# Compression and index scores in one stage, and row maxima taken from masked products

## The reference

```
def compress(k_raw, pe, w1, b1, w2):                   # 31 blocks of 32 tokens, stride 16
    flat = (k_raw[:, idx] + pe).reshape(B, n_cmp, G, 32 * 64)
    return silu(flat @ w1 + b1) @ w2                   # w1: 2048 x 256, w2: 256 x 64

o_cmp: softmax over the 31 compressed keys; o_sel, o_win: softmax over tokens up to t
# index scores of the second kind, 4 heads of 64
logits = einsum('bthd,bsd->bths', qi, ki) / 8
score = einsum('bths,bth->bts', relu(logits), wi / 2)  # masked where s > t
_, idx = top_k(score, 128)                             # the keys that a token attends to
o_dsa = softmax(q @ k[idx] / 8) @ v[idx]
```

## Time and profile before

| | |
|---|---|
| median of 3 runs | 3341.09 us (3338.08 to 3343.44) |
| the profiled execution | 3344.92 us |
| its span, first to last instruction | 3343.1 us |
| mean granted TensorE clock | 0.961 |
| TensorE busy | 3132.5 us (94%) |
| VectorE, ScalarE, GpSimd busy | 1796.5, 857.9, 123.3 us |

### The profile page before, as it was taken

The page is one execution under the profiler, slowest core; times in us unless marked ns, Lnnn a source line. Parts: engine busy times, 40 slices in busy tenths (PEclk is TensorE's granted clock), DMA queues, the critical chain, the costliest instruction groups (busy, mean ns, idle before and its releaser), DMA issues. The chain is left out here.

```text
span 3343.1 us, 42238 instructions
## 1 busy us (share of the span) xinstructions
PE 3132.5 (94%) x17720; PEld 2650.7 (79%) x17720; DVE 1796.5 (54%) x2690; ACT 857.9 (26%) x1051; POOL 123.3 (4%) x96
## 2 busy tenths in 40 slices
PE   7856878999999998999999999999999999899998
PEld 6745436888888886778888888888888886698997
DVE  4647663664655656546545433764645555553434
ACT  3322434421211122314212111421212223132222
POOL 2320221000000000000000000000000000000000
PEclk9975878999999999999999999999999999999999
DMA  4343002343434312113333221342433220232331
GB/s 132 93 121 117 1 0 76 101 126 101 126 113 120 107 45 69 42 51 89 94 94 94 95 60 54 114 145 82 125 101 97 85 68 2 92 89 88 90 96 54
DMA packets 340318, 288.30 MB, mean 86 GB/s; under 512 B 12896, under 2 KB 315488, under 8 KB 339168
## 3 DMA queue, kind: packets, MB, share of 16 engines
q1 hardware_dynamic: 340192, 286.58, 28.8%
HBM read 279.72 MB, written 2.10 MB: 84 GB/s over the span
## 5 line engine op out<-in xcount | busy, mean ns | idle before, releaser
L2117 PE MATMUL PS<-x_hi_f,w_lo 128*128 128x258 f32 (+2 forms) x2560 | 622.3, 324 | 0.0
L2117 PE MATMUL PS<-x_lo_f,w_hi 128*128 128x258 f32 (+2 forms) x2560 | 622.0, 324 | 0.0
L2117 PE MATMUL PS<-x_hi_f,w_hi 128*128 128x258 f32 (+2 forms) x2560 | 620.8, 323 | 0.8 <-DVE w_lo L2165 0.8
L2117 PEld LDWEIGHTS PS<-x_hi_f,w_hi 128*128 128x128 f32 x2560 | 395.4, 189 | 43.9 <-issue 1.5
L2117 PEld LDWEIGHTS PS<-x_hi_f,w_lo 128*128 128x128 f32 x2560 | 395.3, 189 | 42.0
L2117 PEld LDWEIGHTS PS<-x_lo_f,w_hi 128*128 128x128 f32 x2560 | 393.2, 189 | 40.5
L2132 ACT ACTIVATE w_hi<-w_raw 128x2048 fp32r<-128x2048 f32 x131 | 250.0, 1908 | 498.3 <-PE PS L2117 488.8
L2117 PE MATMUL PS<-hid_hi_f,w_hi 128*128 128x512 f32 x1232 | 341.4, 347 | 0.9 <-DVE hid_lo_f L2185 0.9
L2117 PE MATMUL PS<-hid_hi_f,w_lo 128*128 128x512 f32 x1232 | 341.5, 347 | 0.0
L2117 PE MATMUL PS<-hid_lo_f,w_hi 128*128 128x512 f32 x1232 | 339.0, 345 | 0.0
L2143 ACT ACTIVATE silu_a_f<-silu_a_f,shift_out_f 128x512 f32<-128x512 f32 (+1 forms) x154 | 90.2, 626 | 928.7 <-DVE silu_a_f L2176 928.7
(11 more groups left out here) (336 smaller groups left out, 4335.4 us busy)
## 6 DMA issues: line engine op xcount, KB each, us to landing
w_raw<-in_w_ffn_dram SPq DMA_DIRECT2D x240, 512.0 KB, 5.0
sq_f<-in_w_ada_dram SPq DMA_DIRECT2D x128, 512.0 KB, 3.5
w_raw<-in_w_in_dram SPq DMA_DIRECT2D x46, 512.0 KB, 5.0
w_raw<-in_w_out_dram SPq DMA_DIRECT2D x24, 512.0 KB, 5.5
w_raw<-in_w_ffn_dram SPq DMA_DIRECT2D x32, 384.0 KB, 3.9
ada_room<-in_w_ada_dram SPq DMA_DIRECT2D x16, 512.0 KB, 3.4
ada_s<-in_conditions_dram SPq DMA_DIRECT2D x4, 1024.0 KB, 5.0
hT<-hT SPq DMA_DIRECT2D x56, 64.0 KB, 2.0
```

Source lines behind the costliest of these rows:

```text
L2117: last = nc.tensor.matmul(c.PS[:, 4 * q + 2 * w + m, 0:e - a], wt, xt[:, a:e], start=first, stop=end)
```

## The change

- The weights of the key compression are loaded into the ring's two slots at the end of `project_first`. The other tables are loaded at the start of the compression, small ones first; both tables of `attend_first` too.
- `compress` and `index_scores` become one block. The shifted copies are made by ScalarE and VectorE. The hidden product has `G` as stationary operand (64 columns) and `w1` moving (256 columns), one more product with `ones1` adds the bias, and the hidden rows are turned back afterwards. Eight of the twelve score heads are issued between the products of the keys. GpSimd clears `G`.
- Four modulation tiles stay in the compression, twelve go to units 13, 14 and 15 (3, 4, 5), with their loads behind the ring's in SyncE's queue.
- A row item holds several heads where they fit in a bank (`per_row`: 4 heads at 128 keys, 2 at 256, all 8 for `cmp`). TensorE adds the mask by a product with the rounded identity, and VectorE takes a plain maximum. `picked` is now waited for by TensorE.
- Turned maxima lie in the last 128 columns of banks 6 and 7. `back` comes behind the rows of its item and also waits for `moved`. `topk` rounds are dealt out between row items.

```diff
 def project_first(...):                       # SyncE
             for i in range(2, n_steps + 3):
                 if i < n_steps:
                     ring.load(sp, s0 + i, (s0 + i) // 2, (s0 + i) % 2, parts(s0 + i, i))
+                elif i < n_steps + 2:
+                    sp.wait_ge(ring.split, s0 + i + 1)
+                    half = (s0 + i) % 2
+                    sp.dma_start(w1k[:, half * 8:half * 8 + 8, :],
+                                 dram["cmp_k_w1"].rearrange("(j p) n -> p j n", p=P)[:, half * 8:half * 8 + 8, :]).then_inc(c.tally("cmp_wk_in").sem, 16)
                 swap(i - 3)
 def compress(...):                            # TensorE
+                def hidden(i, between):
+                    pe.wait_ge(gathered, i + 1)
...
+                    ps = c.PS[0:GC, 4 + i, 0:CMP_HIDDEN]
+                    nc.tensor.matmul(ps, c.ones1[0:1, 0:GC], b1[:, i], start=True, stop=False)
+                    for j in range(NJ):
+                        last = nc.tensor.matmul(ps, G[:, i, j].rearrange("p g c -> p (g c)"), w1[i][:, j, :], start=False, stop=(j == NJ - 1))
+                        between(j)
+                    last.then_inc(hid_done, 1)
+                def beside_keys(j):
+                    if j % 2:
+                        score(4 + j // 2)
+                def beside_values(j):
+                    if j == 4:
+                        turn_hidden(0)
+                    if j == 9:
+                        output(0, 7)
+                for n in range(4):
+                    score(n)
+                hidden(0, beside_keys)
+                hidden(1, beside_values)
+                pe.wait_ge(normed, 1)
...
+                turn_hidden(1)
+                output(1, 5)
                                               # VectorE
+                gather(0)
...
+                add(0)
+                add(1)
+                gather(1)
+                for n in range(2, len(items)):
+                    add(n)
+                for i in range(len(share.tiles) // 2):
                     share.vector(dve, ch, i)
 class FirstUnit:
-        self.row_items = 1 if branch == "cmp" else HEADS
+        self.per_row = HEADS if branch == "cmp" else min(PER_GROUP, 512 // self.keys)
+        self.row_items = HEADS // self.per_row
 def attend_first(...):                        # TensorE
             def row(i, j):
...
+                wait_bank(pe, n)
+                heads = range(j * u.per_row, (j + 1) * u.per_row)
+                ps = c.PS[:, n % 2, 0:u.per_row * u.keys].rearrange("p (h k) -> p h k", h=u.per_row)
+                for at, h in enumerate(heads):
+                    keys = KKc[:, h // PER_GROUP, :] if u.branch == "cmp" else KK[:, u.kv + h // PER_GROUP, 0:u.keys]
+                    nc.tensor.matmul(ps[:, at, :], Q[:, u.head0 + h, tok], keys, start=(at == 0), stop=False, skip_group_check=True)
                 if u.branch == "cmp":
+                    out, mask = ps, cnegr[:, u.t, None, :].to_broadcast([P, HEADS, CMP_PAD])
+                elif u.branch == "dsa" and u.t > 0:
+                    if j == 0:
+                        pe.wait_ge(picked, u.t)
+                    out, mask = ps[:, 0, :], chosen_mask[:, sc_at[u.t]:sc_at[u.t] + u.keys]
+                    if u.per_row > 1:
+                        out, mask = ps, mask[:, None, :].to_broadcast([P, u.per_row, u.keys])
                 else:
+                    out, mask = ps[:, :, u.t * P:], trir[:, None, :].to_broadcast([P, u.per_row, P])
+                nc.tensor.matmul(out, identr[:], mask, start=False, stop=True, skip_group_check=True).then_inc(rowed, 1)
             def back(i):
...
+                pe.wait_ge(moved, min(i + 4, n_units))
                                               # VectorE
+                    nc.vector.reduce_max(dst, ps, AX_X).then_inc(maxed, 1)
+                    for m in after.get(j, ()):
+                        topk(m)
...
-                early = k // (first[i + 1] - first[i])
+                early = 2 * k // (first[i + 1] - first[i])
...
+                left = range(early, k)
+                after = {j: mine[q * len(mine) // len(left):(q + 1) * len(mine) // len(left)] for q, j in enumerate(left)}
...
+                share.vector(dve, ch, i)
 def first_block(c, dram):
-            share = AdaShare(c.ada, s_c, [room[:, 0], room[:, 1]], room[:, 2], [2] * 8, [(0, 0), (0, 1)])
+            share = AdaShare(c.ada, s_c, bufs, room[:, 2], [1] * 4, ())
...
+            rest = AdaShare(c.ada, s_c, bufs, room[:, 2], [0] * 13 + [3, 4, 5], [(0, 0), (0, 1)], share)
```

More of the change, by code:

```diff
@@ L910, in _, with score @@
-                last.then_inc(out_done.sem, 1)
-                pe.wait_ge(normed.sem, 1)
-                for g in range(GROUPS):
-                    last = nc.tensor.transpose(c.PS[:, 6, g * CMP_PAD:(g + 1) * CMP_PAD], R2[:, g].rearrange("p a d -> p (a d)"), c.ident[0:CMP_PAD, 0:CMP_PAD])
-                last.then_inc(kturned.sem, 1)
+                def score(n):
+                    t, h = items[n]
+                    if n >= 4:
+                        pe.wait_ge(relu, n - 3)
+                    keys = (t + 1) * P
+                    tok = slice(t * P, (t + 1) * P)
+                    half = slice(HD * (h % 2), HD * (h % 2) + HD)
+                    q = HEAD_AT["qi"] + h
+                    nc.tensor.matmul(c.PS[:, n % 4, 0:keys], Q[:, q, tok], KK[:, KI_AT, 0:keys], start=True, stop=False)
+                    nc.tensor.matmul(c.PS[:, n % 4, 0:keys], Q[half, q, tok], KL[half, KI_AT, 0:keys], start=False, stop=True
+                                     ).then_inc(scored, 1)
@@ new lines, in _ @@
+                for i in range(2):
+                    nc.scalar.activation(S[0:HD, i, 0, :], T[0:HD, i, :], ACT.Copy)
+                    nc.scalar.activation(S[HD:P, i, 0, 0:SEQ - 1], T[0:HD, i, 1:SEQ], ACT.Copy).then_inc(stacked, 1)
+                for n, (t, h) in enumerate(items):
+                    act.wait_ge(scored, n + 1)
+                    if n >= 2:
+                        act.wait_ge(added, n - 1)
+                    keys = (t + 1) * P
+                    nc.scalar.activation(R[:, n % 2, 0:keys], c.PS[:, n % 4, 0:keys], ACT.Relu, scale=HD ** -0.5).then_inc(relu, 1)
@@ L1116, in row @@
                 tok = slice(u.t * P, (u.t + 1) * P)
-                wait_bank(pe, "row", i, j)
-                b = bank("row", i, j)
-                if u.branch == "cmp":
-                    for h in range(HEADS):
-                        last = nc.tensor.matmul(c.PS[:, b, h * CMP_PAD:(h + 1) * CMP_PAD], Q[:, u.head0 + h, tok], KKc[:, h // PER_GROUP, :],
-                                                start=True, stop=True)
-                else:
-                    last = nc.tensor.matmul(c.PS[:, b, 0:u.keys], Q[:, u.head0 + j, tok], KK[:, u.kv + j // PER_GROUP, 0:u.keys],
-                                            start=True, stop=True)
@@ L1202, in _ @@
                         row(i + 3, j)
+                if m == 1 and i >= 1:
+                    back(i - 1)
             weigh(len(items) - 1)
```

320 lines of the change are left out of this document (144 added, 176 removed).

## The result

The changed kernel takes 3269.1 us (median of 4 runs, 3267.5 to 3270.5) against 3342.3 us before on the same chip (4 runs, 3338.1 to 3344.9): ratio 0.978, 95% interval 0.977 to 0.980. The forecast was 3259.0 with a range of 3240 to 3295. The profiled execution has a span of 3267.7 us, 75.4 less than before.

A forecast was written before the change was run, and what follows sets the result against it. The prediction took chains of waits, with no engine always full and TensorE's clock low, to bound the attention part. Terms -54.5 - 1.5 - 36.4 + 10.3 = -82.1 us, from the 3341.1 median, gave 3259.0; range 3240 to 3295.

The forecast's parts named there:

- rival C: Compression: TensorE stays at 1.2 GHz; saving there only 42 us, time 3271 us; chance 0.12.
- rival A: Whole kernel: the forecast as summed from its terms, 3259 us, own range 3243 to 3280; chance 0.62.
- Term 1: Compression and index scores, merged into one stage: next stage starts at 264.3 instead of 318.8, -54.5 us.
- I take cold to 235 (6.3 us of the work), then half time: Compression, keys with eight scores: 27 us at 1.2 GHz, clock doubling from 235, so they end at 245.4.
- The hidden product: Compression: one product of 256 moving columns against 64-column weights takes 0.96 us at 1.2 GHz, 0.48 at 2.4.
- Term 2: Start of the attention: no late tables or shared-bank stall, 15.7 us for 17.2, -1.5 us.
- Term 3: Attention units 0 to 12: fewer waits between TensorE and VectorE, 133.5 us for 169.9, -36.4 us.
- rival B: Attention: VectorE and TensorE trade waits as before, saving 10 us or less there; 3285 us, up to 3295; chance 0.16.
- 5.5 us: Attention units: grouping heads cuts VectorE's reductions from 36.7 to 31.2 us over 13 units, saving 5.5 us.
- the masks' 7.7: Attention units: about 60 mask matmuls added on TensorE cost 7.7 us.
- the order: Attention units: dealt-out top-k rounds, separate columns for turned maxima and back-turn behind rows were held to bring what remains.
- Term 4: Last three attention units: twelve modulation tiles moved onto VectorE there delay the last finish, +10.3 us.

The follow-up runs named there:

- light tiles: The changed kernel with the twelve modulation tiles of the last three units cut to 64 of 1024 columns, leaving the modulation incomplete: 3259.2 us, ratio 0.975.

## Why the prediction was right, and where it was not

The time lies in the range, 10 us above 3259.0, and the direction and most of the terms came as forecast. The mechanism did not in the compression: there the clock of rival C ruled, and C's 3271 is nearer to the 3269.1 than the 3259 of rival A. Of the signs named ahead of the result, those that hang on this failed: TensorE was not at 2.4 GHz by 240, the attention's first product came at 275.3, not at 264 to 266, and the turn in unit 13 at 426.7, not near 414. The others came, or nearly: TensorE's longest wait for maxima was 2.6 us, the last finish came 43.9 us behind the turn for 42, and no turn waited for the row banks, though one waited 2.3 us for a finish in the banks that it now shares.

- **Term 1, -54.5 forecast, -46.3 measured.** This is the largest miss. The step that failed is "I take cold to 235 (6.3 us of the work), then half time". Counted from the start of the stage, the keys and their scores took 27.0 us for the 16.7 of the forecast (+10.3), the gather was 1.8 us quicker, and the rest 0.3 quicker. The price of a product and the 27 us for keys and scores at 1.2 GHz came out to within 0.1 us; rival C, "the compression stays at 1.2 GHz", is what happened until 260. Its stage would be 54.7 us long; measured are 50.3, as the gather was quicker and the clock rose in the values. What I left out is that eight of the products between are of half height. In the run without them the keys end at 245.4, the number of the forecast, but that is in part a coincidence: that stage began 2.7 us later, and its scores are also cheaper, by the loads that no longer stand between. I looked to the earlier trace rows for what raises the clock, long moving operands, and not to the scores' own stage in the earlier trace rows, 14.84 of 16.80 us busy at 0.50.
- **The hidden product.** 0.96 forecast from the old row, 0.95 measured. The Trainium skill's rule that the next weights load while a matmul runs (TensorE: Matmul & The Clock Gate, what happens on issuing a matmul), by which it would be 0.85, is not borne out by these. It does hold for the full-height score products, 0.12 us apart with a load of 0.19 each.
- **Term 2** -1.5, as forecast.
- **Term 3, -36.4 forecast, -34.1 measured,** and with it rival B falls. But its inside was off. For the first four units the block of rounds is shown to be the cause. For units 4 to 9 I gave grouping "5.5 us" on VectorE, less than the masks' 7.7, and held "the order" to be the gain; the runs showed the reverse: grouping is worth 9 to 15 there with the masks on TensorE, the block 0.8 to 3.5, the new order nothing. The 5.5 us also leave out the 81 accumulator reads behind the fused operations of the earlier trace rows; VectorE's busy time fell by 8.4. In units 10 to 12 I was 4.3 too high, and the grouping's 2.0 and the block's 0.6 leave most of their 6.8 without a shown cause. The row bank's wait that went is a candidate, and the granted clock there rose from 0.63 to 0.85, where the forecast had 6 us for a low clock. The reduction's price, 0.69 for the 0.68 of the forecast, was right.
- **Term 4, +10.3 forecast, +12.1 measured.** The mechanism is shown by the light tiles. Mis-sized are the tiles, 37.9 us for 34.7: their work of 2.6 us is right, and so are the late loads in sum (4.4 us, where pairs of 6.0 allow for 4.8), but one operation in each unit takes 2.16 to 2.18 us instead of 1.23. The finishes between were shorter than forecast, which gives some of it back.
- **The sum.** By its terms the forecast was 12.3 us too low, 8.2 + 2.3 + 1.8. The stage began 2.0 us later, and 7.7 us less went by in unchanged code: 6.6 us too low between the two profiled executions. The other 3 us come from the medians: the profiled execution before lay 3.8 us above its median, which the forecast took off, and the one after only 0.7. The 7.7 us were not forecast, and lie within what executions of such kernels differ by. That the time is only 10 us off, and not some 18, is luck.

## What to carry to other kernels

Before dense work is priced at the higher clock, look at what a stage with the same mixture of shapes was granted: here products of 64 and 128 rows in turn ran 0.19 us further apart, and the clock stayed low until they were made equal. Work moved to an idle engine is free only where it stands in that engine's order at the very place of the idle time: two tiles more in units 10 to 12 cost 6.3 us, with 3.3 us idle in one piece elsewhere in VectorE's order. Where two engines hand small items to and fro, fewer and larger items can be worth more than the saved work of either engine alone (11.7 us for 8.0 and 4.1 here, from one pair of traces).

## What the hardware showed beyond the forecast

- Alternating heights: products of 256 columns 0.31 us apart at full granted clock, 0.12 with equal heights.
- The clock can fall under full load: in the run with the scores behind the keys it went from 1.00 to 0.53 in the window from 242, some 5 us after the half-height products began, with no idle moment on TensorE.
- VectorE's tile operation with two inputs from SBUF took 2.16 to 2.18 us instead of 1.23 once in each of the last units, while GpSimd works on the finish of the unit; GpSimd's operation took 2.15 to 2.20 us beside the tiles and 1.28 behind them. With light tiles the same operation of VectorE took 1.26 to 1.31 us instead of 0.22, so the loss is about 1 us whether it has 1024 columns or 64: it looks like a wait, not like a slower rate. A copy of 64 x 512 at the stage's start took 2.04 us beside GpSimd's fill of the gather buffer, and 0.42 alone (order of time of the run with the scores behind the keys); that the fill is the cause is not tested:

```profile
222.10 2.04 DVE L1014 COPY hT<-cmp_t 64x512 f32<-64x512 f32 x1 [0.33 <-PEq L663]
...
228.74 0.42 DVE L1014 COPY hT<-cmp_t 64x512 f32<-64x512 f32 x1
```

- The same instructions of units 4 to 9 took 54.9, 58.3 and 61.2 us at granted clocks of 0.97, 0.90 and 0.86.
